# Paged-cache attention steps of a hybrid decoder: one piece of a dense projection moved to between two groups of small matmuls

## The chip, the cores and the metric

The kernel runs on 1 core of one Trainium2 chip. The metric is the device time of the whole launch in microseconds (us). The kernel is written engine by engine: TensorE (PE), VectorE (DVE), ScalarE (ACT), GpSimd (POOL) and SyncE (SP) each have an instruction list, and semaphores order them.

## What is computed

One layer of a decoder over 512 prompt tokens (with 16 meta tokens ahead) and 8 running sequences. Every layer has a gated-linear-attention group and a latent-attention group, then an output projection and a SwiGLU FFN. The change touches two parts: the attention of the 8 running sequences over their paged caches (4096 positions each), and the dense projections of the normed input into queries, keys and values of the linear-attention group.

```python
def page_step(carry, pages):                       # over the 32 pages of each sequence
    ck, kp = cache_ckv[layer, pages], cache_kpe[layer, pages]
    sc = (q_lat . ck + q_pe . kp) * MLA_SCALE      # scores, 4 heads
    m_new = maximum(m, sc.max(-1)); p = exp(sc - m_new)
    acc = acc * exp(m - m_new) + p @ ck            # values are the latent rows again
q, k, v, gr, g, cq, ckv, kpe = split(n @ w_in)     # q, k, v: the "dense pieces" below
```

## The kernel before

**The cache steps.** The caches are worked on in 16 steps, two for each of the 8 sequences (STEPS = 16). A step reads two halves, each of 128 partitions x 2048 latent elements (tile KC, 1 MB) and 128 x 512 rotary elements (KP, 256 KB), which POOL gathers from HBM by indirect DMA (L662 for KC, L669 for KP; the small copy L654 ahead of each pair writes the row numbers). They lie in a ring of six buffers, that is three steps. For half h, `gather_latent(h)` waits until the transposes of half h-6 are done and until the values matmuls of its step are done (semaphore pv_done, L661). So the two gathers of KC that POOL issues in step n are released by the values matmuls of step n-1, which PE runs inside step n.

Per step n the engines do this:

- DVE, in this order: `latent_keys(2n+1)` (L1911, transposes KC into KT), `rope_keys(2n+1)` (L1919, KP into KTp), `rope_keys(2n+2)` (waits for the scores of half 2n, since it writes their KTp), in steps 2, 7 and 13 also `lo(...)` (L1808, 2.25 us, the low part of the next weight block), then `cache_max(n)` (L1950 and L1952: the maximum over the scores, after both halves' scores), `latent_keys(2n+2)`, and `cache_probs(n)` (L1961, probabilities spread out for the values matmuls, writes PS).
- ACT: evacuates dense tiles that are complete, then `cache_exp(n)` (L1546, writes Pc after `cache_max(n)`).
- PE: two pieces of a dense projection, `cache_scores(n, 0)` (L991: 40 fp32 matmuls on tiles of 128x32, which the trace has as 80), `cache_values(n-1)` (L1014: 16 matmuls, 32 in the trace, also 128x32), `cache_scores(n, 1)`, then one or two more dense pieces, then `cache_spread(n)` (L1000: 4 matmuls of 128x128, after `cache_exp(n)`). The matmul that ends a group of scores raises sc_done, on which `cache_max` waits.

**The dense pieces.** `dense_piece(k)` is six matmuls, a part of a query, key (L934 to L936) or value (L815 to L817) tile. 92 pieces in all; pieces 0 to 15 run ahead of the steps, and `before_spread(n)` says how many are done before the spread of step n: three or four a step. They fill PE while it waits for DVE and ACT. Their matmuls use the whole 128x128 array.

**What sets the order.** Nothing but the text: the loop at L1018 to L1029 is PE's order, and PE runs it as it stands. DVE's, ACT's and POOL's orders are loops of their own and wait by semaphores.

```python
for n in range(STEPS):
    dense_piece(k)
    dense_piece(k + 1)
    cache_scores(n, 0)
    if n:
        cache_values(n - 1)
    cache_scores(n, 1)
    for k in range(k + 2, before_spread(n)):
        dense_piece(k)
    cache_spread(n)
    k = before_spread(n)
```

Of the kernel before, what the change touches and what calls it, by code (L numbers as in the profile page):

```python
# [240 lines left out]
def before_spread(n):  # L241

    return 16 + 4 * n + 4 - (n + 2) // 2 if n < STEPS else PIECES
# [13 lines left out]
def hybrid_decode_kernel(nc, ins, outs):  # L257
# [6 lines left out]
    with ExitStack() as ctx:  # L264
# [187 lines left out]
        def S(name):  # L452
            return signals[name]
# [302 lines left out]
        def _(pe):  # L756
# [220 lines left out]
            def cache_scores(n, y):  # L977

                if y == 0:
                    pe.wait_ge(S("kt_done"), 2 * n + 1)  # L980
                else:
                    pe.wait_ge(S("kt_first"), n + 1)
                if y == 0 and n >= 2:
                    pe.wait_ge(S("ps_done"), n - 1)
                o = 512 * (n % 2) + 64 * y
                for c in range(NBLK):
                    if y == 1 and c == 8:
                        pe.wait_ge(S("kt_done"), 2 * n + 2)
                    for t in range(NG):
                        kk = KT[y][:, 2 * t:2 * t + 2, c, :] if c < 8 else KTp[y][:, 2 * t:2 * t + 2, c - 8, :]  # L990
                        ins = mm(pairs[2][32 * t:32 * t + 32, o:o + 64], Qall[:, n // 2, 32 * c:32 * c + 32], kk, start=c == 0, stop=c == NBLK - 1)  # L991
                ins.then_inc(S("sc_done"), 1)

            def cache_spread(n):

                pe.wait_ge(S("sc_free"), n + 1)
                o = 512 * (n % 2) + P
                first16 = ident.rearrange("p (t a c) -> p a t c", t=NG, a=2)
                for v in range(4):
                    ins = nc.tensor.transpose(pairs[2][:, o + 64 * v:o + 64 * v + P], Pc[:, v, :, :].rearrange("p g j -> p (g j)"), first16)  # L1000
                ins.then_inc(S("sp_done"), 1)

            def cache_values(n):

                b = n // 2
                o = 512 * (b % 2)
                if n % 2 == 0 and b >= 2:
                    pe.wait_ge(S("ov_free"), b - 1)
                pe.wait_ge(S("ps_done"), n + 1)
                for v in range(4):  # L1010
                    x = (2 * n + v // 2) % RING
                    for t in range(NG):
                        unit = 2 * t + v % 2
                        ins = mm(pairs[3][32 * t:32 * t + 32, o:o + KVL], PS[n % 2][:, 4 * v + t, :], KC[x][:, KVL * unit:KVL * unit + KVL],  # L1014
                                 start=n % 2 == 0 and v == 0, stop=n % 2 == 1 and v == 3)
                ins.then_inc(S("pv_done"), 1)

            k = 16  # L1018
            for n in range(STEPS):
                dense_piece(k)  # L1020
                dense_piece(k + 1)
                cache_scores(n, 0)
                if n:
                    cache_values(n - 1)
                cache_scores(n, 1)
                for k in range(k + 2, before_spread(n)):
                    dense_piece(k)
                cache_spread(n)
                k = before_spread(n)  # L1029
# [1297 lines left out]
```

## Time and profile before

| | us |
|---|---|
| median of 3 runs | 880.56 |
| lowest, highest | 875.74, 881.65 |
| the profiled execution | 876.61 |
| its span, first to last instruction | 874.8 |
| PE busy | 794.5 (91%) |
| DVE busy | 445.6 (51%) |
| ACT busy | 270.6 (31%) |
| POOL busy | 124.1 (14%) |

The cache steps are the stretch from 111.3 us to about 290 us; ahead of them lie the norms and first projections, behind them prompt attention, the output projection and the FFN, where PE is busy without a break from 500 to 800 us. Times in the rows are from the first instruction. A PE row is the time at which the matmul was issued to the array and a modelled end, and PE rows run on while later ones wait; the releasers are read from semaphores.

### The profile page before, as it was taken

How to read it: one execution, taken by the hardware profiler on the slowest of the kernel's cores; microseconds unless marked ns; L12 is line 12 of the kernel's file. 1: busy time of each engine (PE TensorE's matmuls, PEld its weight loads, DVE VectorE, ACT ScalarE, POOL GpSimd, SP SyncE). 2: the span in 40 equal slices, each digit the busy share in tenths (PEclk: the TensorE clock that was granted, in tenths of full speed). 3: DMA queues.
4: the chain of work that ended last, by engine and by line, in shares of the span. 5: the costliest groups of instructions: out<-in, count | busy, mean ns of one | idle time of the engine just before them, and what ended most of it. 6: DMA issues, size and time to landing. Idle time of an engine off the chain costs nothing.

```text
span 874.8 us, 20180 instructions
## 1 busy us (share of the span) xinstructions
PE 794.5 (91%) x8841; PEld 750.6 (86%) x8841; DVE 445.6 (51%) x593; ACT 270.6 (31%) x429; POOL 124.1 (14%) x153
## 2 busy tenths in 40 slices
PE   2999888677769799999999999999999999999996
PEld 1999777566657589788999999999999999999996
DVE  5365567455557647779544555544445445123123
ACT  5346211111111534446534422222222223123213
POOL 6201414323332003622000000000000000000000
PEclk9999989978899999779999999999999999999999
DMA  9525556746763120231621322233333322322202
GB/s 260 170 56 175 214 210 244 262 153 238 290 242 137 49 73 5 57 97 51 200 84 47 105 83 78 87 95 96 96 96 96 96 85 67 114 97 85 84 0 97
DMA packets 72672, 106.52 MB, mean 122 GB/s; under 512 B 7808, under 2 KB 64216, under 8 KB 68384
## 3 DMA queue, kind: packets, MB, share of 16 engines
q1 hardware_dynamic: 64912, 63.42, 23.1%
q0 software_dynamic: 7696, 42.15, 13.1%
q8 instruction: 52, 0.85, 0.4%
q14 instruction: 12, 0.10, 0.0%
HBM read 101.03 MB, written 4.00 MB: 120 GB/s over the span
## 4 chain that ended last, share of the span: by engine, by line
PE 82%; DVE 5%; another core or an unknown queue 4%; issue 4%; ACT 3%; DMA 1%; SPq 0%; ACTq 0%; DVEq 0%
PE pair L797 10%; PE pair L799 10%; PE pair L798 10%; PE pair L782 8%; PE pair L784 8%; PE pair L783 8%; PE pair L991 4%; PE pair L1014 2%; PE pair L1213 1%; PE pair L815 1%; PE pair L817 1%; PE pair L816 1%; PE pair L835 1%; PE pair L1000 1%
## 5 line engine op out<-in xcount | busy, mean ns | idle before, releaser
L797 PE MATMUL pair<-xhi,whi 128*128 128x260 f32 x736 | 209.1, 284 | 0.4 <-ACT rsf L1736 0.4
L799 PE MATMUL pair<-xhi,wlo 128*128 128x260 f32 x736 | 208.5, 283 | 0.0
L798 PE MATMUL pair<-xlo,whi 128*128 128x260 f32 x736 | 208.5, 283 | 0.0
L797 PEld LDWEIGHTS pair<-xhi,whi 128*128 128x128 f32 x736 | 139.5, 190 | 0.7 <-issue 0.6
L798 PEld LDWEIGHTS pair<-xlo,whi 128*128 128x128 f32 x736 | 139.5, 190 | 0.0
L799 PEld LDWEIGHTS pair<-xhi,wlo 128*128 128x128 f32 x736 | 139.3, 189 | 0.0
L784 PE MATMUL pair<-hhi,wlo 128*128 128x260 f32 x352 | 99.4, 282 | 0.0
L782 PE MATMUL pair<-hhi,whi 128*128 128x260 f32 x352 | 99.3, 282 | 0.0
L783 PE MATMUL pair<-hlo,whi 128*128 128x260 f32 x352 | 99.2, 282 | 0.0
L1911 DVE STREAM_TRANSPOSE KT<-KC 128x2048 uint32<-128x2048 uint32 x32 | 73.7, 2302 | 0.0
L2266 DVE TENSOR_TENSOR wlo<-wraw,whi 128x2048 fp32r<-128x2048 f32 x22 | 50.4, 2293 | 38.7 <-ACT whi L1756 38.7
L782 PEld LDWEIGHTS pair<-hhi,whi 128*128 128x128 f32 x352 | 66.3, 188 | 0.0
L783 PEld LDWEIGHTS pair<-hlo,whi 128*128 128x128 f32 x352 | 66.2, 188 | 0.0
L784 PEld LDWEIGHTS pair<-hhi,wlo 128*128 128x128 f32 x352 | 66.1, 188 | 0.0
L2291 DVE TENSOR_TENSOR wlo<-wraw,whi 128x2048 fp32r<-128x2048 f32 (+1 forms) x10 | 20.8, 2079 | 75.9 <-ACT whi L1768 75.9
L1751 ACT ACTIVATE hhi<-fe 128x520 f32 x22 | 13.8, 640 | 106.7 <-DVE fe L2279 106.7
L662 POOL DMA_INDIRECT KC<-in_cache_ckv,icur x32 | 31.7, 992 | 103.7 <-PE pair L1014 98.0
L1000 PE MATMUL pair<-cst,Pc 128*128 128x128 f32 x64 | 13.0, 334 | 33.8 <-ACT Pc L1546 26.2
L991 PEld LDWEIGHTS pair<-KT,Qall 128*32 128x32 f32 x2048 | 36.7, 121 | 8.2 <-issue 4.4
L991 PE MATMUL pair<-KT,Qall 128*32 128x64 f32 x2048 | 40.8, 235 | 2.0 <-issue 1.7
L1000 PEld LDWEIGHTS pair<-cst,Pc 128*128 128x128 f32 x64 | 8.2, 164 | 39.8 <-ACT Pc L1546 31.5
L1756 ACT ACTIVATE whi<-wraw 128x2048 fp32r<-128x2048 f32 x22 | 41.8, 1901 | 0.0
(362 smaller groups left out, 1687.1 us busy)
## 6 DMA issues: line engine op xcount, KB each, us to landing
wraw<-in_w_gate SPq DMA_DIRECT2D x11, 1024.0 KB
wraw<-in_w_up SPq DMA_DIRECT2D x11, 1024.0 KB
wraw<-in_w_down SPq DMA_DIRECT2D x8, 1024.0 KB
X<-in_x_prompt SPq DMA_DIRECT2D x8, 512.0 KB, 5.7
wraw<-in_w_in SPq DMA_DIRECT2D x4, 1024.0 KB
wsame<-in_w_in SPq DMA_DIRECT2D x4, 1024.0 KB
wraw<-in_w_down SPq DMA_DIRECT2D x4, 768.0 KB
wsame<-in_w_out SPq DMA_DIRECT2D x2, 1024.0 KB
```

The costliest lines, as they stand in the source:

```text
L662: g.indirect_dma_start(KC[x][:, :], None, ckv_rows, bass.IndirectOffsetOnAxis(icur[x][:, 0:1], 0)).then_inc(S(f"kc_loaded{x}"), 16)
L782: mm(out, wcols(h, j), hi[:, kx, tok], start=first and j == 0, stop=False)
L783: mm(out, wcols(h, j), lo[:, kx, tok], start=False, stop=False)
L784: ins = mm(out, wcols(l, j), hi[:, kx, tok], start=False, stop=last and j == len(k_of) - 1)
L797: mm(out, h[:, k, c], xhi[:, k, tok], start=k == order[0], stop=False)
L798: mm(out, h[:, k, c], xlo[:, k, tok], start=False, stop=False)
L799: ins = mm(out, l[:, k, c], xhi[:, k, tok], start=False, stop=k == order[-1])
L991: ins = mm(pairs[2][32 * t:32 * t + 32, o:o + 64], Qall[:, n // 2, 32 * c:32 * c + 32], kk, start=c == 0, stop=c == NBLK - 1)
L1000: ins = nc.tensor.transpose(pairs[2][:, o + 64 * v:o + 64 * v + P], Pc[:, v, :, :].rearrange("p g j -> p (g j)"), first16)
L1756: f(whi[n % 2][:, :], wraw[n % 2][:, :], ACT.Copy).then_inc(w_hi, 1)
L1911: v_.transpose(KT[y][:, :, :, :].rearrange("p u c j -> p (u c j)").bitcast(U32), KC[x][:, :].bitcast(U32)).then_inc(S(signal), 1)
L2266: tt(wlo[n % 2][:, :], wraw[n % 2][:, :], whi[n % 2][:, :].bitcast(F32), ALU.subtract).then_inc(w_lo, 1)
```

## The change

In PE's loop the second of the two dense pieces at the head of each step goes from ahead of `cache_scores(n, 0)` to behind `cache_values(n - 1)`, just ahead of `cache_scores(n, 1)`. In step 0, which has no values, it stands between the two groups of scores.

```diff
             for n in range(STEPS):
                 dense_piece(k)
-                dense_piece(k + 1)
                 cache_scores(n, 0)
                 if n:
                     cache_values(n - 1)
+                dense_piece(k + 1)
                 cache_scores(n, 1)
                 for k in range(k + 2, before_spread(n)):
                     dense_piece(k)
```

On PE, at the middle of step 1, this is the place where the piece arrives (whi and wlo are the weight block, xhi and xlo the input, KT0/KTp0 and KT1/KTp1 the keys of the two halves, KC the values):

```order
@@ -579,4 +579,8 @@
 L935 MATMUL pair0<-xlo_50,whi1_52 128x268
 L936 MATMUL pair0<-xhi_49,wlo1_54 128x268
+L991 MATMUL pair2<-KT0_93,Qall_73 32x64 x32
+L991 MATMUL pair2<-KTp0_95,Qall_73 32x64 x8
+L1014 MATMUL pair3<-KC0_81,PS0_97 32x256 x8
+L1014 MATMUL pair3<-KC1_82,PS0_97 32x256 x8
 L934 MATMUL pair0<-xhi_49,whi1_52 128x268
 L935 MATMUL pair0<-xlo_50,whi1_52 128x268
```

The first half's scores and the values of the step before now come six dense matmuls earlier. On PE again, a few rows on, where the second half's scores begin:

```order
@@ -585,8 +589,4 @@
 L935 MATMUL pair0<-xlo_50,whi1_52 128x268
 L936 MATMUL pair0<-xhi_49,wlo1_54 128x268
-L991 MATMUL pair2<-KT0_93,Qall_73 32x64 x32
-L991 MATMUL pair2<-KTp0_95,Qall_73 32x64 x8
-L1014 MATMUL pair3<-KC0_81,PS0_97 32x256 x8
-L1014 MATMUL pair3<-KC1_82,PS0_97 32x256 x8
 L991 MATMUL pair2<-KT1_94,Qall_73 32x64 x32
 L991 MATMUL pair2<-KTp1_96,Qall_73 32x64 x8
```

There the dense piece stands directly ahead of the second half's scores, where the values stood before. No instruction is added or removed, and the lists of DVE, ACT, POOL and SP are the same as before.

## Rows read from the trace of the kernel before

**Rows 1.** Windows: two cache steps; busy us of each engine, then PEclk, DMA, GB/s.

```profile
160.20:173.70 13.50, 9.35 (x220) 8.06 (x220) 7.76 (x8) 1.11 (x5) 4.60 (x7) 0.87 0.66 235
...
269.10:277.30 8.20, 7.08 (x214) 5.95 (x214) 7.01 (x8) 1.42 (x4) 0.98 (x2) 1.00 0.82 309
```

**Rows 2.** Waits, 108 to 292 us: who waited for whom, us in total, times, longest.

```profile
POOL KC L662 <- PE pair L1014: 98.0, 13, 16.1
...
DVE fin L1950 <- remote: 47.4, 9, 7.1
```

**Rows 3.** Timeline of step 5: start, us, engine, line, idle before and releaser.

```profile
164.98 1.90 PE L1014 MATMUL pair<-KC,PS 128*32 128x256 f32 x32
...
166.71 1.07 PE L991 MATMUL pair<-KT,Qall 128*32 128x64 f32 x62
...
167.65 0.40 PE L991 MATMUL pair<-KTp,Qall 128*32 128x64 f32 x14
...
167.69 0.95 POOL L662 DMA_INDIRECT KC<-in_cache_ckv,icur  x1 [7.14 <-PE pair L1014]
...
171.23 0.29 DVE L1950 TENSOR_REDUCE fin<-pair 128x1 f32<-128x128 f32 x1 [5.21 <-remote]
```

**Rows 4.** Timeline of step 14, which issues no gather behind its values.

```profile
274.92 0.41 PE L991 MATMUL pair<-KTp,Qall 128*32 128x64 f32 x16
...
275.40 0.29 DVE L1950 TENSOR_REDUCE fin<-pair 128x1 f32<-128x128 f32 x1 [1.16 <-PE pair L991]
```

**Rows 5.** Timeline of steps 1, 2, 8 and 12: first gather and cache_max of each.

```profile
122.43 0.95 POOL L662 DMA_INDIRECT KC<-in_cache_ckv,icur  x1 [16.07 <-PE pair L1014]
...
125.95 0.29 DVE L1950 TENSOR_REDUCE fin<-pair 128x1 f32<-128x128 f32 x1 [4.87 <-remote]
...
134.53 1.32 POOL L662 DMA_INDIRECT KC<-in_cache_ckv,icur  x1 [7.00 <-PE pair L1014]
...
136.01 0.29 DVE L1950 TENSOR_REDUCE fin<-pair 128x1 f32<-128x128 f32 x1 [0.98 <-PE pair L991]
...
203.91 0.95 POOL L662 DMA_INDIRECT KC<-in_cache_ckv,icur  x1 [3.76 <-PE pair L1014]
...
209.72 0.29 DVE L1950 TENSOR_REDUCE fin<-pair 128x1 f32<-128x128 f32 x1 [7.14 <-remote]
...
253.34 0.95 POOL L662 DMA_INDIRECT KC<-in_cache_ckv,icur  x1 [5.63 <-PE pair L1014]
...
257.62 0.29 DVE L1950 TENSOR_REDUCE fin<-pair 128x1 f32<-128x128 f32 x1 [5.08 <-remote]
```

**Rows 6.** Timeline of PE in step 1, in and out of the small-tile matmuls.

```profile
118.23 0.28 PE L935 MATMUL pair<-xlo,whi 128*128 128x268 f32 x1
118.35 0.29 PE L936 MATMUL pair<-xhi,wlo 128*128 128x268 f32 x1
118.57 1.10 PE L991 MATMUL pair<-KT,Qall 128*32 128x64 f32 x64
...
122.33 0.41 PE L991 MATMUL pair<-KTp,Qall 128*32 128x64 f32 x16
122.67 0.39 PE L934 MATMUL pair<-xhi,whi 128*128 128x268 f32 x1
122.89 0.29 PE L935 MATMUL pair<-xlo,whi 128*128 128x268 f32 x1
```

**Rows 7.** Timeline of step 12, where the second half's scores are late.

```profile
254.37 0.43 PE L991 MATMUL pair<-KTp,Qall 128*32 128x64 f32 x15
```

**Rows 8.** Timeline of DVE and PE at the head of step 14.

```profile
268.21 2.31 DVE L1911 STREAM_TRANSPOSE KT<-KC 128x2048 uint32<-128x2048 uint32 x1
...
269.15 0.66 PE L1000 MATMUL pair<-cst,Pc 128*128 128x128 f32 x4 [0.71 <-ACT Pc L1546]
...
271.16 1.04 PE L991 MATMUL pair<-KT,Qall 128*32 128x64 f32 x60
```

**Rows 9.** The line of the latent gathers, whole run.

```profile
DMA to landing us min/median/max: 6.1/7.3/8.6
```

## Prediction

> **What bounds the kernel now.** I read the page first: PE is busy 91% of the span, but in its slices of 22 us the cache steps stand out, where PE is at 6 to 8 tenths. So I cut that stretch into windows, one per step. They come in two kinds [rows 1]: a step of the first kind takes 13.5 us for 9.35 us of PE work, one of the last three takes 8.2 us for 7.08 us. The work is the same. What differs is that the first kind issues gathers and the last ones do not (the latent halves 6 to 31 are gathered during steps 1 to 13, two a step).
>
> The waits say who is late [rows 2]. POOL's latent gathers wait 98 us for the values matmuls, and DVE's `cache_max` waits 47.4 us in nine steps for a releaser that the profile cannot match. The timeline of step 5 shows why it cannot [rows 3]. The values matmuls end at 164.98 + 1.90 = 166.88. The second half's scores are issued from 166.71 and end, by their rows, at 167.65 + 0.40 = 168.05. `cache_max` needs nothing else, yet starts at 171.23, 3.18 us later. In step 14, where no gather is issued, the same pair of rows gives 275.33 and 275.40, a lag of 0.07 us [rows 4]. So the scores' completion is held back in steps with gathers, and I call that time the hold.
>
> The hold is timed by POOL, not by PE. From the start of the first latent gather to `cache_max` it is 171.23 - 167.69 = 3.54 us in step 5 [rows 3] and 125.95 - 122.43 = 3.52 us in step 1 [rows 5]. Steps 1, 3, 4, 5, 6, 9, 10 and 11, eight in all, look alike. Step 8 has 5.81 us and step 12 has 4.28 us [rows 5]. In steps 2, 7 and 13 DVE is still on `lo` when the gather starts, the gather takes 1.32 us instead of 0.95, and the lag is only 136.01 - 134.53 = 1.48 us [rows 5]. Ten steps have the long hold; steps 0, 2, 7, 13, 14 and 15 do not.
>
> The path of a step is therefore: spread, the two dense pieces, scores, values, scores, the hold, `cache_max`, `cache_exp`, the next spread. All PE work ahead of the hold is on the path in series. The dense pieces behind the second scores hide under the hold and the ACT and DVE work.
>
> **The change, part by part.**
>
> *The piece itself.* It stays ahead of the second scores, so its six matmuls are on the path before and after. At full clock they follow each other by 118.35 - 118.23 = 0.12 us [rows 6], that is 6 x 0.12 = 0.73 us with rounding. Their net cost is nothing.
>
> *More changes between large and small tiles.* Before, a step goes from 128x128 matmuls to 128x32 ones and back once; after, twice. Going in costs 118.57 - 118.35 = 0.22 us where 0.12 is the pitch, so 0.10 [rows 6]. Coming out, the last small matmul starts at about 122.52 (122.33 + 0.41 less 0.22, a small matmul's length in the trace), a next one would follow in 0.05, and the dense one starts at 122.67: 0.10 more. The second dense matmul then comes after 0.22 instead of 0.12: again 0.10 [rows 6]. Together 0.30 us per step, and 16 x 0.30 = 4.8 us if every step pays it on the path. The Trainium skill, "TensorEngine Tiling (Array Packing)", section Key Properties, says that changing the tiling mode drains TensorE. If each of the two added changes waits out the rest of one dense matmul (0.29 less 0.12 us, from the same rows), that gives 0.34 us per step and 5.4 us; this rule speaks against the change, and the trace agrees with it in size.
>
> *The values end earlier.* They are issued six dense matmuls sooner, 0.73 us at full clock. Where the granted clock is at half (1.2 GHz) over that whole piece, it is up to twice that, 1.46 us. POOL starts its gather 167.69 - 166.88 = 0.81 us after them [rows 3], so the gather starts 0.73 us earlier too. At that moment PE has just finished the moved piece, and the second scores, 1.2 to 1.3 us of work, fall wholly behind the gather's start. Before, only about 0.4 us of them did.
>
> *What the hold then does* is the unknown term. No row has this exact order, so I bound it by neighbours. From below: `cache_max` still comes 3.52 us after the gather starts, so it comes 0.73 us sooner. From above: as in step 8, 5.81 us after it, so 5.81 - 3.52 - 0.73 = 1.56 us later. Nearest to the new order is step 12, where the scores' last rows end at 254.37 + 0.43 = 254.80, which is 1.46 us behind the gather's start at 253.34 [rows 5, 7]; after the change I expect about 0.73 - 0.81 + 1.30 + 0.30 = 1.5 us. There the lag was 4.28 us: 4.28 - 3.52 - 0.73 = +0.03 us per step. I take that value.
>
> *The keys of the first half come closer.* In step 14 the spread starts at 269.15 and the scores at 271.16 [rows 8]; with one piece less they want to start at 270.43. Their transpose ends at 268.21 + 2.31 = 270.52. So about 0.1 us may be lost ahead of the first scores; it is won back, as the same time is then missing ahead of the second. I count nothing, and up to 0.1 x 16 = 1.6 us as bound.
>
> *Gathers.* Issued sooner by 0.73 us, they land in 7.3 us [rows 9] and are transposed no earlier than a whole step, at least 8.2 us [rows 1], later. DVE's transposes L1911 wait for no landing in the steps. Nothing is won there. In steps 2, 7 and 13 `lo` and the gather both move ahead by about as much, so they still overlap; if they did not, these three would get the long lag, 3 x (3.52 - 1.48) = 6 us.
>
> *Sum.* Ten hold steps at +0.03 give +0.3 us, their tile changes being under the hold; six other steps at +0.30 give +1.8 us. The profiled execution took 876.61 us, so 876.61 + 2.1 = 878.7 us. The median of the runs shown is 3.95 us above that execution; on its scale the forecast is 880.56 + 2.1, rounded to 882.5 us.
>
> **The rivals.**
>
> 1. *The hold has a fixed end, 3.52 us behind the gather.* For it: eight steps of ten agree to 0.06 us, although their scores were not all equally far. Against it: the two steps whose scores were latest broke it. Time: 10 x (-0.73) + 1.8 = -5.5 us, 875.1 us; with the piece at half clock throughout, 10 x (-1.46) + 1.8 = -12.8, 867.8 us.
> 2. *The hold has a fixed length behind the scores' own end.* Then only the tile changes count, in all 16 steps: +4.8 us, 885.4 us. For it: the lag is near 3.2 us in most. Against it: steps 8 and 12 have less behind their own ends.
> 3. *The hold gets longer, as in step 8.* What decides is how much of the second scores lies behind the gather's start: 0.4 us in step 5, all of it after the change. If that stretches every hold as in step 8, it is 10 x 1.56 + 1.8 = +17.4 us, 898.0 us. For it: step 8 itself. Against it: step 12, whose lateness is the nearer to the new order's, lost less.
> 4. *The hold disappears*, because it needs values and scores in one unbroken stretch. Then each of ten steps gains up to 3.1 us, less 4.8 us of tile changes: -26 us, 854.6 us. DVE would allow it, as the 8.2 us step shows. The steps with `lo` speak for it weakly, since there too the hold is cut when something on another engine shifts.
>
> **How the numbers follow.** I give the forecast 0.36, rival 1 0.21 (0.05 of it at half clock), rival 2 0.16, rival 3 0.15, rival 4 0.07, and 0.05 to the rest. Runs of before spread from 875.74 to 881.65, so about 1% (8.8 us) is what a measurement can tell from no change. Faster by over 1%: rival 4, the half-clock part of rival 1 and a little of the rest, 0.14. Slower: rival 3 and some of the rest, 0.18. Same: 0.68. The range 872 to 894 holds the forecast, rival 2, rival 1 at full clock and a third of rival 3; left out are rival 4, the far end of rival 1 and the worse part of rival 3, about 0.2.
>
> **What would show it.** In the changed profile, six dense rows should stand between L1014 and the second L991 of each step, and L662 should start about 0.8 us behind the end of L1014. Right if the lag from the first L662 to L1950 is 4.1 to 4.5 us in the ten steps and 1.5 us in steps 2, 7 and 13. Near 3.5 us is rival 1, near 5.8 us is rival 3, under 2 us is rival 4. If the lag from the scores' rows to L1950 is 3.2 us everywhere, it is rival 2. In steps 0, 14 and 15 the time should grow by 0.3 us each; if it does not, the tile changes are mis-sized. Wrong altogether if the last kind of step gets shorter, for then PE's series was not the path.

## The result, and the profile after

| us | before | changed |
|---|---|---|
| median of the comparison | 881.07 | 899.68 |
| lowest, highest | 875.74, 881.65 | 897.93, 901.46 |
| span of the profiled execution | 874.8 | 896.9 |

The ratio is 1.0206, with a 95% interval from 1.0163 to 1.0249. The forecast was 882.5 us and no measurable change, the range ended at 894: the prediction is wrong. The time nearest to the measured one is that of rival 3, 898.0 us. The medians differ by 18.6 us and the two profiled executions by 22.1 us (876.61 and 898.68), because the profiled one of before is 4.5 us under its median; what is read from the traces below adds up to the second figure.

There is a second half to this result. On most other chips the same pair of kernels goes the other way. The study is about both.

First the windows of the changed kernel, a step with gathers (step 4) and the one without (step 14), from spread to spread; the columns are those of [rows 1]. The first line is step 4 of before.

```profile
148.50:160.20 11.70, 8.15 (x216) 6.94 (x214) 6.45 (x8) 1.64 (x5) 4.23 (x7) 0.91 0.89 315
...
155.00:168.30 13.30, 10.40 (x216) 7.81 (x214) 5.15 (x8) 1.78 (x4) 4.23 (x6) 0.88 0.48 170
290.60:299.50 8.90, 7.70 (x214) 6.48 (x214) 6.48 (x8) 1.44 (x4) 1.30 (x2) 1.00 0.83 308
```

PE's busy time in step 4 grew from 8.15 to 10.40 us although no instruction was added, and the step without gathers takes 8.9 us where it took 8.2 [rows 1]. The waits from 108 to 310 us, as in [rows 2]:

```profile
POOL KC L662 <- PE pair L1014: 119.1, 13, 15.3
DVE fin L1950 <- PE pair L991: 79.1, 14, 7.8
...
PEld pair L991 <- issue: 41.6, 77, 0.6
...
PE pair L991 <- issue: 29.2, 72, 0.4
```

`cache_max` no longer waits for a releaser that the profile can't match. It waits for L991 itself, and L991 stops 72 times inside its own group, for nothing that the profile shows, 0.4 us at most each time. The timeline of step 4 shows how:

```profile
159.24 0.83 PE L1014 MATMUL pair<-KC,PS 128*32 128x256 f32 x12
...
160.72 0.28 PE L936 MATMUL pair<-xhi,wlo 128*128 128x268 f32 x1
160.88 0.95 POOL L662 DMA_INDIRECT KC<-in_cache_ckv,icur  x1 [9.76 <-PE pair L1014]
...
160.94 0.87 PE L991 MATMUL pair<-KT,Qall 128*32 128x64 f32 x46
...
162.16 0.34 PE L991 MATMUL pair<-KT,Qall 128*32 128x64 f32 x5 [0.35 <-issue]
...
162.92 0.34 PE L991 MATMUL pair<-KT,Qall 128*32 128x64 f32 x5 [0.42 <-issue]
...
163.67 0.34 PE L991 MATMUL pair<-KT,Qall 128*32 128x64 f32 x6 [0.42 <-issue]
...
164.99 0.98 POOL L669 DMA_INDIRECT KP<-in_cache_kpe,icur  x1 [0.27 <-POOL icur L654]
...
166.69 0.24 PE L991 MATMUL pair<-KTp,Qall 128*32 128x64 f32 x1 [0.43 <-issue]
...
166.98 0.29 DVE L1950 TENSOR_REDUCE fin<-pair 128x1 f32<-128x128 f32 x1 [7.00 <-PE pair L991]
```

The values end at 160.07, the gather follows 0.81 us later, and the rows of 46 of the 80 small matmuls follow without a stop. From then on PE gets five or six through every 0.75 us, until 166.69; POOL's four gathers last until 164.99 + 0.98 = 165.97. I call this the trickle. From the first gather to `cache_max` it is 166.98 - 160.88 = 6.10 us. In steps 1, 3 to 6 and 8 to 12 the lag lies between 6.08 and 6.30 us; step 7 has 3.97. In steps 2 and 13, where `lo` lengthens the first gather, it stays short:

```profile
136.39 1.69 POOL L662 DMA_INDIRECT KC<-in_cache_ckv,icur  x1 [10.05 <-PE pair L1014]
...
138.27 0.29 DVE L1950 TENSOR_REDUCE fin<-pair 128x1 f32<-128x128 f32 x1 [1.02 <-PE pair L991]
```

The account of the loss has four parts, each the difference between the two traces. The lags of steps 1 to 13 grew by 26.4 us in all. The stretches from a spread to the next first latent gather shrank by 12.3 us, a little more than 13 pieces of 0.73 us. The stretches from `cache_max` to the next spread grew by 7.6 us. Steps 14 and 15, which have no gather behind their values, grew by 0.67 and 0.37 us (from one first L1000 row to the next, 8.22 to 8.89 and 8.92 to 9.29). The sum is 22.8 us, and from the spread of step 0 to that of step 15 the stage grew from 170.2 to 193.0 us.

The third part is one that the prediction had put under the hold. The dense pieces behind the second scores now stand behind the trickle, and they run at the lower of the two clocks. In step 1 they begin at 127.31, `cache_max` at 127.42, and the granted clock of the window behind is 0.50:

```profile
127.31 0.59 PE L934 MATMUL pair<-xhi,whi 128*128 128x268 f32 x1
127.42 0.29 DVE L1950 TENSOR_REDUCE fin<-pair 128x1 f32<-128x128 f32 x1 [6.60 <-PE pair L991]
```

```profile
127.30:130.10 2.80, 2.80 (x13) 2.79 (x13) 2.64 (x3) 0.78 (x2) 0.00 (x0) 0.50 0.91 376
```

Twelve of them, 0.22 us apart where they are 0.12 apart at full clock, keep PE busy until the spread at 130.16, 2.74 us after `cache_max`. In step 1 of before the same stretch is 1.35 us long and PE has nothing left to do in it. So it is in steps 1, 3, 9 and 11, 4.7 of the 7.6 us. In steps 6, 7 and 13, 3.2 us, `cache_exp` itself starts later, and why I have not traced.

### The profile page after: what moved, and what is told of

Read it like the earlier page. It is cut to its first block, busy times and chain, and to the rows that moved or that the text cites. A ratio compares the mean times of both kernels' runs of the same rounds, so it can differ in the third digit from the quotient of the medians.

```text
span 896.9 us, 20180 instructions
## 1 busy us (share of the span) xinstructions
PE 819.7 (91%) x8841; PEld 759.9 (85%) x8841; DVE 445.4 (50%) x593; ACT 270.4 (30%) x429; POOL 124.9 (14%) x153
## 4 chain that ended last, share of the span: by engine, by line
PE 86%; issue 5%; DVE 3%; ACT 2%; another core or an unknown queue 2%; DMA 1%; SPq 0%; ACTq 0%; DVEq 0%
PE pair L797 10%; PE pair L799 10%; PE pair L798 10%; PE pair L782 8%; PE pair L784 8%; PE pair L783 7%; PE pair L991 7%; PE pair L1014 3%; PE pair L815 2%; PE pair L816 2%; PE pair L817 2%; PE pair L1000 1%; PE pair L1213 1%; PE pair L1145 1%
## 5 line engine op out<-in xcount | busy, mean ns | idle before, releaser
L797 PEld LDWEIGHTS pair<-xhi,whi 128*128 128x128 f32 x736 | 139.2, 189 | 0.7 <-issue 0.6
L991 PE MATMUL pair<-KT,Qall 128*32 128x64 f32 x2048 | 48.9, 229 | 17.7 <-issue 17.7
L991 PEld LDWEIGHTS pair<-KT,Qall 128*32 128x32 f32 x2048 | 36.5, 115 | 29.8 <-issue 26.1
L1950 DVE TENSOR_REDUCE fin<-pair 128x1 f32<-128x128 f32 x16 | 4.7, 292 | 82.6 <-PE pair L991 79.1
L815 PE MATMUL pair<-whi,xhi 128*128 128x256 f32 x120 | 42.6, 355 | 0.4 <-issue 0.4
```

The costliest lines, as they stand in the source:

```text
L797: mm(out, h[:, k, c], xhi[:, k, tok], start=k == order[0], stop=False)
L815: mm(out, hi[:, tok], wcols(h, j), start=j == 0, stop=False)
```

## Experiments

The hypotheses at the start: **A**, while GpSimd issues gathers, PE gets small matmuls through only in a trickle; **C**, it is the gathers' traffic; **D**, the added tile changes (from 128x128 matmuls to 128x32 ones and back) cost the whole 18 us. **B**, the order of the work as such, came beside them. Later came **F**, that PE waits for its own instructions.

The stage is the time from the first L1000 matmul of step 0 to that of step 15. The last column is worked out from the traces and explained further down: the breaks of more than 0.5 us from one matmul row to the next for which the profile shows no releaser and which end at the edge of a block of PE's instructions, behind a packet that brings instructions. Both columns are of the one profiled execution, which in after_third took 838.04 us, 6.8 us less than its median.

| kernel | chip | us | ratio to before, interval | stage | such breaks, us |
|---|---|---|---|---|---|
| before, changed | first | 881.07, 899.68 | 1.0206, 1.0163 to 1.0249 | 170.2, 193.0 | 6.0, 0 |
| late_gather | 7 | 847.74 | 1.0009, 0.9972 to 1.0046 | 146.1 | 18.7 |
| late_gather_moved | 7 | 842.69 | 0.9940, 0.9900 to 0.9979 | 141.9 | 15.3 |
| piece_before_values | 7 | 845.82 | 0.9966, 0.9936 to 0.9997 | 145.3 | 17.8 |
| small_gather | 7 | 835.09 | one execution | 132.9 | 5.7 |
| before_again | 13 | 848.41 | | 145.5 | 20.2 |
| after_again | 13 | 844.38 | 0.9964, 0.9939 to 0.9989 | 143.8 | 13.8 |
| hardware_loads | 13 | 848.58 | 1.0012, 0.9980 to 1.0044 | 144.8 | 15.6 |
| half_the_small_matmuls | 13 | 830.93 | one execution | 132.3 | 10.1 |
| half_the_columns | 13 | 841.90 | 0.9932, 0.9891 to 0.9973 | 140.8 | 14.2 |
| after_fourth | 13 | 841.29 | 0.9934, 0.9892 to 0.9976 | 140.2 | 13.5 |
| after_third | 6 | 844.81 | 0.9984, 0.9955 to 1.0012 | 139.2 | 13.6 |
| late_gather_moved_second | 6 | 844.49 | 0.9953, 0.9928 to 0.9977 | 142.9 | 14.5 |
| late_gather_moved_third | 8 | 846.17 | 0.9971, 0.9942 to 1.0000 | 142.5 | 12.9 |
| after_fifth | 10 | 898.06 | 1.0274, 1.0197 to 1.0350 | 191.7 | 1.0 |
| small_gather_timed | 10 | 898.54 | 1.0278, 1.0208 to 1.0348 | 192.1 | 0.8 |
| small_gather_before | 10 | 877.92 | 0.9995, 0.9963 to 1.0028 | 170.1 | 2.0 |
| late_gather_moved_fourth | 10 | 875.09 | 0.9893, 0.9822 to 0.9965 | 169.9 | 0.9 |
| hardware_loads_second | 9 | 848.48 | 0.9691, 0.9636 to 0.9746 | 145.1 | 15.1 |

The kernel before itself took 849.64 us on chip 7, 848.41 and 849.26 on 13, 847.37 on 6, 847.29 on 8, but 878.76 and 883.13 on 10 and 874.10 on 9. So there are two kinds of chip for this kernel. I call 6, 7, 8 and 13 ordinary, and 9, 10 and that of the first measurement the trickling kind. The kernel before itself was traced on the first chip and on 13 only; elsewhere its time tells which kind a chip is. Of the 28.2 us between the spans of before_again and of the first trace, 24.7 lie in the stage (145.5 against 170.2).

### A later gather, and another place for the piece

In late_gather the latent gather waits for the second scores too (order of before); late_gather_moved has the same in the changed order. piece_before_values leaves the gather and puts the piece between the first scores and the values; its lines below are against the changed kernel.

```diff
                     pool.wait_ge(S("pv_done"), (h - RING) // 2 + 1)
+                    pool.wait_ge(S("sc_done"), 2 * ((h - RING) // 2 + 1) + 2)
```

```diff
                 cache_scores(n, 0)
+                dense_piece(k + 1)
                 if n:
                     cache_values(n - 1)
-                dense_piece(k + 1)
                 cache_scores(n, 1)
```

> The order of before; POOL's first latent gather of a step waits for the second half's scores too, not only for the values. Theory A (while POOL issues its gathers, PE gets through small matmuls only at about five in 0.75 us, so what counts is how many of them lie behind the first gather's start): no score is left behind the gather, the lag from the scores' last row to cache_max falls from 3.2 us to under 0.2 us in the ten hold steps, and the kernel is 20 to 30 us faster than before. Theory B (the hold comes from the order of matmuls on PE, wherever POOL is): the lag stays at 3 us, no change. Theory C (the transferred data slow PE, not their issue): the transfers now meet the next step's first scores, so these get longer by what the second scores gain, no change within 5 us.

> The same late gather, with the piece moved as in the change. Theory A: the change then costs only its two added changes between large and small tiles, 0.3 us in 16 steps: 4 to 6 us slower than the late gather with the order of before, and still clearly faster than before. Theory B: it stays 18 us slower than its partner, and the second scores take 6 us from the gather's start. Theory D (the tile changes themselves cost the 18 us): the same 18 us.

> The moved piece stands between the first half's scores and the values, so values, second scores and gathers keep before's order and distance, but the two added tile changes are there. Theory A: the hold is as before, 3.5 us from gather to cache_max; only 0.3 us x 16 = 5 us are lost. Theory D (tile changes): about as slow as the change, +18 us.

All three ran on chip 7, where by its time the kernel before has next to no hold to remove, so A's 20 to 30 us, its hold of 3.5 us and its cost of 4 to 6 us all missed, and the three say little on A, B and C. late_gather is no different from before, 1.0009. late_gather_moved is 0.6% faster. piece_before_values is 0.3% faster, with lags from 0.69 to 2.69 us, where 3.5 was the pattern of the first trace. What they did show: an order with more tile changes in every step does not cost 18 us by itself (piece_before_values 0.9966, late_gather_moved 0.9940), and steps 14 and 15 of the first comparison agree (0.67 and 0.37 us). D fell.

### A quarter of the gathers' bytes

```diff
-                g.indirect_dma_start(KC[x][:, :], None, ckv_rows, ...)
+                g.indirect_dma_start(KC[x][:, 0:512] if h >= RING else KC[x][:, :], None,
+                                     kpe_rows if h >= RING else ckv_rows, ...)
```

> The changed kernel, but the latent gathers of halves 6 to 31 read rows of 512 elements instead of 2048, so POOL issues as many gathers of as many rows with a quarter of the latent bytes; three quarters of the values and keys are stale. Theory A: the second scores still take 5 us or more from the gather's start. Theory C (traffic): that time falls to under 3 us.

> The order of the changed kernel; from the seventh half on the latent gathers fetch rows of 512 elements from the rotary cache in place of 2048 from the latent cache (a quarter of the bytes, the same number of gathers), so the latents of those halves are not the reference's. Theory F (TensorE waits for its own instructions, because their packets come late behind the gathers' traffic): 833 to 838 us and under 6 us of such waits in the cache steps. If it is the issuing of gathers by GpSimd, whatever their size, 842 to 845 as in the changed kernel.

> The order of the kernel before, with the same small gathers. Theory F: the waits for instruction packets fall from 18 us to under 7 us, so it takes 830 to 838 us, and the changed order has lost its advantage: small_gather_timed against this one lies between 0 and +0.7% (16 pieces with four tile changes more a step, 0.30 us each, are 4.8 us, 0.6%). If the advantage of the changed order has nothing to do with those waits, this kernel is 0.2 to 0.7% slower than small_gather_timed.

The latents of these halves are not the cache's, so this is a kernel for timing only. On chip 7 the changed order took 835.09 us with them, in one execution; the changed kernel itself was not timed there, and on the other ordinary chips it took 841 to 845. Its lags are 1.41 to 2.24 us. This misses A's 5 us and looks like C's "under 3", but the changed kernel on an ordinary chip has 1.42 to 4.17 us (after_again), so there was no trickle to remove. On chip 10 nothing happened: 898.54 against 898.06 us in the changed order, 877.92 against 878.76 in the order of before. What was expected of the last two runs, made for an ordinary chip, missed, so for F small_gather's one execution is the only run with fewer bytes. (The second expectation counts four added tile changes a step; there are two, for 0.30 us together.) The timeline of step 4 of small_gather_timed has the same trickle:

```profile
157.39 0.95 POOL L662 DMA_INDIRECT KC<-in_cache_kpe,icur  x1 [9.10 <-PE pair L1014]
...
157.45 0.87 PE L991 MATMUL pair<-KT,Qall 128*32 128x64 f32 x46
...
159.44 0.33 PE L991 MATMUL pair<-KT,Qall 128*32 128x64 f32 x5 [0.42 <-issue]
...
160.17 0.33 PE L991 MATMUL pair<-KT,Qall 128*32 128x64 f32 x6 [0.40 <-issue]
...
163.43 0.29 DVE L1950 TENSOR_REDUCE fin<-pair 128x1 f32<-128x128 f32 x1 [6.79 <-PE pair L991]
```

Five or six per 0.73 us, and a lag of 6.04 us, at a DMA rate of 92 GB/s from 108 us to the end of the stage in place of 201. Over the stage GpSimd's queue moved 13.4 MB in 4080 packets in place of 33.8 MB in 5744. C is refuted for the trickle, as far as it is a matter of bytes.

### The two kernels again

> The kernel before, unchanged, profiled on the chip on which the other experiments run. On that chip the kernel before took 849.64 us in 25 executions, 31 us less than in the first profile, whose rows carry the prediction. Theory A (while GpSimd issues its four gathers, TensorE gets through only about five small matmuls in 0.75 us) says that the 31 us lie in the cache steps: the lag from the first gather of a step to cache_max, 3.5 us in eight of the first fifteen steps, should be under 1.5 us here, and the sixteen steps together 20 to 30 us shorter. Theory D (the machine is just faster as a whole) says that the lags stay at 3.5 and that every stage is about 3.5% shorter.

> The changed kernel, unchanged, on the same chip. If what the change costs is the time that small matmuls lose behind a gather's start (theory A), it costs there as much as that loss is present on this chip: between -0.5% (none of it: the six later pieces only fill other places) and +2% (as in the first measurement), with the lag of the first gather to cache_max above that of the kernel before in most steps. If it is the eight tile changes a step themselves (theory D: 18 us over 16 steps, whatever GpSimd does), it is +2% here too, 867 us, and the kernel with the same order and a later gather, which took 0.994 of the time before, would not have come out so.

> The changed kernel, unchanged, on whichever chip this job gets. Theory M (what the change costs depends on how much small matmuls are slowed behind a gather's start, and that differs between chips): if the kernel before takes 870 to 885 us here, the change costs 1.5 to 2.5% and the lags from first gather to cache_max are about 6.1 us in ten steps; if the kernel before takes about 849 us, it costs between -1% and 0 and most lags are 1.4 to 3.2 us. Rival (the +2% of the first measurement comes with the order of the work, and the second measurement at 0.996 was the odd one): +1.5 to +2.5% here wherever the kernel before stands.

> The changed kernel, unchanged, beside half_the_columns. If the kernel before takes about 849 us here, the changed kernel takes 0.994 to 1.001 of it, as on the three chips so far; if it takes 870 to 885, the ratio is 1.015 to 1.025 and the lags from the first gather to cache_max are about 6.1 us.

> The changed kernel, unchanged. If the kernel before takes about 849 us here, the changed kernel takes 0.993 to 0.999 of it; if it takes 870 to 885, the ratio is 1.015 to 1.025, with ten lags of about 6.1 us.

On ordinary chips the changed kernel is 0.9964, 0.9984 and 0.9934 of the kernel before: a gain of 0.2 to 0.7%, of which one interval takes in 1. On chip 10 it is 1.0274, with lags of 5.92 to 6.06 us in steps 1 and 3 to 12. The first measurement was no accident, and the sign of this change depends on the chip. The interval on chip 10 overlaps with that of the first measurement. Two of the expected ratios were narrowly missed: 0.9934 where 0.994 to 1.001 was expected, and 1.0274 where 1.015 to 1.025 was; both intervals reach into the expected range. In before_again the stage was 24.7 us shorter, as A expected, but only nine of its thirteen lags are under 1.5 us; the other four are taken up below.

### Holding the gather back on a trickling chip

> The order of the changed kernel, the latent gather held back until the second half's scores are done, on the same chip as after_third. Theory A (GpSimd's issuing of gathers slows the small matmuls behind it): 840 to 848 us on any chip, because no small matmul of the scores stands behind a gather's start; on a chip where the kernel before takes 870 to 885 that is a ratio of 0.955 to 0.975, elsewhere 0.99 to 1.0. Rival (the chip is slower as a whole): the ratio to the kernel before is 0.99 to 1.0 on every chip, so 870 or more where the kernel before takes 880.

> The order of the changed kernel, the latent gather held back until the second half's scores are done. Where the kernel before takes 870 to 885 us: theory A (GpSimd's issuing of gathers slows small matmuls behind it) expects 842 to 855 us, a ratio of 0.96 to 0.98, and scores that end 0.1 us before cache_max in every step; a rival (such a chip slows the cache steps' matmuls as such, or only moves the slow time behind the new place of the gather) expects 0.99 to 1.02. Where the kernel before takes about 849 us: 0.993 to 0.998, as on chips 7 and 6.

> The same kernel as late_gather_moved_third, for a chip of the slower kind. Where the kernel before takes 870 to 885 us: theory A expects 842 to 855 us and scores that end 0.1 us before cache_max; the rival (the slow time only moves behind the gather's new place) 0.99 to 1.02 of the kernel before. Where the kernel before takes about 849 us: 0.993 to 0.998.

The second and third ran on ordinary chips (0.9953, 0.9971), the fourth on chip 10: 875.09 us, 0.9893 of the kernel before. My expectation of 842 to 855 us was wrong, and the rival, that the slow time only moves, came nearest with its 0.99 to 1.02. The timeline of its steps 3 and 4 (line numbers are one higher here) shows it. The first gather has started at 148.40, behind the scores of step 3. The first half's scores of step 4 begin at 150.40:

```profile
150.40 1.13 PE L992 MATMUL pair<-KT,Qall 128*32 128x64 f32 x43
...
151.10 0.95 POOL L663 DMA_INDIRECT KC<-in_cache_ckv,icur  x1 [0.30 <-issue]
...
151.96 0.32 PE L992 MATMUL pair<-KT,Qall 128*32 128x64 f32 x6 [0.43 <-issue]
...
152.53 0.97 POOL L670 DMA_INDIRECT KP<-in_cache_kpe,icur  x1 [0.27 <-POOL icur L654]
152.72 0.33 PE L992 MATMUL pair<-KT,Qall 128*32 128x64 f32 x5 [0.43 <-issue]
...
153.46 0.32 PE L992 MATMUL pair<-KT,Qall 128*32 128x64 f32 x5 [0.41 <-issue]
...
154.35 0.37 PE L992 MATMUL pair<-KTp,Qall 128*32 128x64 f32 x12
```

The trickle is now in the other half's scores, behind the second latent gather. It stops at about 154.3, 0.8 us after the end of the last gather, 152.53 + 0.97, and the rows that are left follow without a stop. This is the closest view of A: the trickle moved with the gathers and ended with them. That it is shorter because only some of the gathers meet small matmuls is my reading. The view has a limit. Gathers are being issued from 148.40 on, yet 43 rows from 150.40 on show no stop (46 in step 4 of the changed kernel), and since PE's rows can run ahead of its completions, the rows do not tell when the slowing begins. The stage is 169.9 us, where the changed kernel has 191.7 on this chip.

### No gathers by GpSimd

hardware_loads has the changed order. The loops of gathers on POOL are gone; ScalarE issues plain transfers of the same size at the matching points: in both traces the first KC transfer of a step is issued 0.4 to 0.8 us after the values end, ahead of the second half's scores. The kernel leaves out the page table and reads the rows in the order of the cache.

```diff
+            def load_half(h):
+                x = h % RING
+                act.dma_start(KP[x][:, :], flat_kpe[P * h:P * h + P, :]).then_inc(S(f"kp_loaded{x}"), 16)
+                act.dma_start(KC[x][:, :], flat_ckv[P * h:P * h + P, :]).then_inc(S(f"kc_loaded{x}"), 16)
...
+                if 1 <= n <= 13:
+                    act.wait_ge(S("pv_done"), n)
+                    for h in (2 * n + 4, 2 * n + 5):
+                        act.wait_ge(S("kt_done"), h - RING + 1)
+                        load_half(h)
```

> The order of the changed kernel; latents and rotary rows of all halves are loaded by plain transfers that ScalarE issues (the same bytes into the same buffers, at the same points: after the step's scores and transposes), and GpSimd issues no gather in the cache steps. It reads the rows in their order in the cache, without the page table, so the values differ from the reference's. Theory A (what slows small matmuls is GpSimd issuing indirect transfers): the lag of the first load to cache_max is that of the matmuls alone, below 1.6 us, no groups of five with gaps, and the time is 25 us or more under the kernel before's of the first profile, at 0.98 to 0.995 of the kernel before on the same chip. Theory C (the traffic of 0.6 MB into SBUF slows TensorE's reads): the lags stay as in the changed kernel on this chip, and the time too.

> The same kernel as hardware_loads: the changed order, rows loaded in their order in the cache by transfers that ScalarE issues, no gather of GpSimd in the cache steps, so the values differ from the reference's. Where the kernel before takes 870 to 885 us: if the slow matmuls come with GpSimd's issuing, 843 to 855 us, a ratio of 0.96 to 0.98, and no scores in groups of five or six; if they come with any transfer into these buffers, 890 to 900 us with such groups. Where the kernel before takes about 849 us: 0.998 to 1.005, as on chip 13.

On ordinary chip 13: 848.58 us, 1.0012. On chip 9, where the kernel before took 874.10 us: 848.48 us, 0.9691 with an interval from 0.9636 to 0.9746. With the same bytes into the same buffers but no gathers from GpSimd, the kernel takes the same time on either kind of chip. This settles A against C. What it leaves open is whether the engine that issues counts or the kind of transfer (indirect gathers against plain ones, over another queue), since both changed together. The timeline of step 4 on chip 9, the transfers and the scores (L979 here):

```profile
149.86 0.34 ACTq L1521 DMA_DIRECT2D KP<-in_cache_kpe  x1
150.22 1.36 ACTq L1522 DMA_DIRECT2D KC<-in_cache_ckv  x1
```

```profile
150.60 1.10 PE L979 MATMUL pair<-KT,Qall 128*32 128x64 f32 x64
151.52 0.41 PE L979 MATMUL pair<-KTp,Qall 128*32 128x64 f32 x16
```

All 80 in one run, straight behind two transfers. From the first KC transfer to `cache_max` it is 1.77 us here and 1.46 to 1.86 in the other steps without a break (A had expected less than 1.6). In the whole stage of this trace PE makes no stop of over 0.5 us without a releaser but the ten in the table's last column. The changed kernel itself was not timed on chip 9, so the 3.1% are against the kernel before. On chip 13, hardware_loads is about as slow as before, though the changed order alone is 0.4 to 0.7% faster (it was expected at 0.98 to 0.995); what ScalarE's issuing costs there was not traced. (The 0.6 MB in the first expectation is a slip: a half is 1.25 MB.)

### Where the ordinary chips lose and gain

The trace of before_again raised a new question: its lags run from 0.68 to 3.36 us, and PE has a few long breaks instead of a trickle. Its PE rows in steps 5 and 10:

```profile
158.22 0.61 PE L991 MATMUL pair<-KT,Qall 128*32 128x64 f32 x27
161.14 0.55 PE L991 MATMUL pair<-KT,Qall 128*32 128x64 f32 x25 [2.31 <-issue]
```

```profile
210.66 0.28 PE L816 MATMUL pair<-whi,xlo 128*128 128x256 f32 x1
213.10 0.37 PE L817 MATMUL pair<-wlo,xhi 128*128 128x256 f32 x1 [2.16 <-issue]
```

The second break is between two dense matmuls, so it has nothing to do with tile size. The DMA view of a short window at each place, 158.6 to 158.7 and 210.70 to 210.75, shows what else started:

```profile
q8 instruction: 1, 0.02, 68.7%
```

```profile
q8 instruction: 1, 0.02, 126.0%
```

In each it is one packet of the instruction queue, 16 KB (0.85 MB in 52 packets over the whole run). By the trace these two start at 158.64 and 210.72, and PE is back 2.50 and 2.38 us later. PE waits for its own instructions there, because it has used them up before the next packet has come (F). The trace shows it in a second way. Between the first L1000 rows of steps 0 and 15 PE has 6547 rows, counted with weight loads and the few other instructions of its list, and 26 packets of queue 8 start: about 252 rows to a packet, so 256 is the natural count. Number PE's rows from the first, and take every break of over 0.5 us that has no releaser. In the 14 traces without a trickle there are 143 of them, and every one ends at row 193 or 194 of a block of 256. 133 of the 143 end 2.2 to 2.6 us after a packet starts, the rest within 2.1 to 3.1 us. The short stops of the trickle are another thing: of the 72 in the changed kernel's first trace not one ends so behind a packet. These sums are the last column of the table. The step has two groups of 80 matmuls with 160 instructions in 1.3 us each, weights and matmuls, with only the values between them in the old order.

The Trainium skill, "Runtime: NRT & Kernel Launch", section Instruction fetch mechanics, says that crossing to a new 16 KiB block is mostly hidden. Here the trace disagrees: 13 to 20 us of the stage on ordinary chips, with the full gathers or loads.

Two kernels in the changed order test F. Both leave out half of the second half's scores. half_the_small_matmuls makes them with half of the matmuls (five of ten blocks, 40 of 80 in the trace; the expectation says nine and 72, which is a slip), half_the_columns keeps their number and halves their columns.

```diff
-                for c in range(NBLK):
+                for c in (range(NBLK) if y == 0 else (0, 1, 2, 3, 8)):
```

```diff
+                        if y == 1:
+                            ins = mm(pairs[2][32 * t:32 * t + 32, o:o + 32], Qall[:, n // 2, 32 * c:32 * c + 32], kk[:, 0:1, :], ...)
+                            continue
```

> The order of the changed kernel; the second half's scores are made of five of nine contraction blocks (40 small matmuls of 72; the first half's stay), so that part of the scores is left out. Theory A, with n matmuls left behind the first gather's start at 0.15 us each (0.75 us for five): where the lag of the changed kernel on this chip is above 1.5 us, it falls by nearly half. Theory B (the order of the work alone; the lag is a fixed wait after the gather, whatever stands behind it): the lag stays.

> The order of the changed kernel; each matmul of the second half's scores takes 32 columns in place of 64, so half of the keys of that half get no scores, but the number of TensorE's instructions stays. Theory F (in the cache steps TensorE waits for its own instructions: on the three chips so far its longest gaps end 2.3 to 2.5 us after a 16 KB packet of the instruction queue starts, and the steps with 144 instructions in 1.1 us use a packet up faster than that): the gaps stay, and the time is within 0.5% of the changed kernel's 842 to 845 us, where half the matmuls gave 830.9. Rival (TensorE's time in the scores sets the end): halving the columns gives what halving the matmuls gave, 830 to 836 us.

Half the columns: 841.90 us beside the changed kernel's 841.29 on the same chip, breaks 14.2 us beside 13.5, as F expects. The columns are not free, since steps 14 and 15 became 0.43 and 0.42 us shorter (8.14 and 8.87 beside 8.57 and 9.29); why the whole did not become shorter I have not traced. Half the matmuls: 830.93 us in one execution, 10.4 to 13.5 us under the changed kernel on that chip, and breaks 10.1 us, only 3.4 to 3.7 us less. The larger part is work in series: a lag without a break is 0.90 us in place of 1.44, and 16 x 0.54 is 8.6 us, an estimate. So this run fits F and is no proof of it. The same fits the table: with a quarter of the gathers' bytes on chip 7 the breaks are 5.7 us instead of 13.5 to 13.8. There the traffic counts, unlike for the trickle. That the packets then come sooner was not measured by itself.

F also fits the gain on ordinary chips. The dense piece between values and second scores spreads PE's instructions: breaks 20.2 and 18.7 us in the old order, 13.8, 13.5 and 13.6 in the new. The stage is 145.5 and 146.1 us in the old, 139.2 to 143.8 in the new. But the tile changes cost something as well: steps 14 and 15 grew by 0.34 and 0.33 us on chip 13. They did not cost that in every step. Steps 4 and 6 have gathers and no break in either trace of that chip (before_again, after_again), and they grew by 0.07 and 0.04 us only. With one trace to a run, and 1.7 to 6.3 us between their stages, the account of the gain is a fit and not shown. On trickling chips such breaks are 0 to 6 us in all kernels with gathers.

## Why the prediction was wrong, step by step

- **The path of a step** had the hold in series on it, and that was right: the grown lags show up in the stage. Its last sentence was not. The dense pieces behind the second scores were to hide under the hold, and in the changed kernel they ran behind `cache_max`, at a granted clock near 0.50 in most steps: 4.7 us of the 7.6 us that these stretches grew. Two smaller readings were off as well: the page has PE at 9 tenths in the slice from 262 to 284 us, not at 6 to 8, and 13.5 us is the longest of the steps with gathers, which run from 10.05 to 13.44.
- **The piece at no cost**: six dense rows stand between L1014 and the second L991, and the gather starts 0.81 us behind the values, as before. Right.
- **Tile changes, 0.30 us a step**: measured 0.67 and 0.37 in steps 14 and 15 of the first comparison, 0.34 and 0.33 on chip 13. Slightly low for a step without gathers. The rule of the Trainium skill ("TensorEngine Tiling (Array Packing)", Key Properties), worked out there as 0.34 us, as an estimate hits the figures of chip 13. That these changes hide under the hold in steps with gathers was given without a reason, as they lie ahead of the gather's start. Chip 13 has +0.07 and +0.04 us in two such steps, so there they hardly cost anything; for the trickling chips it is not shown.
- **What the hold then does, +0.03 us a step**, is the step that failed. The lag was to be 4.1 to 4.5 us and was 6.08 to 6.30. In step 4 that is 6.10 - 3.53 - 0.73 = +1.84 us instead of +0.03; over the ten steps the lags grew by 23.5 us, which less ten times 0.73 is +1.62 us a step (step 8 had -0.35, because its lag was 5.81 us already in the kernel before). Two things were wrong in it. I took the neighbour by the time at which the scores' last row ends, and step 12 looked nearest. But step 12's rows were late by a break of 1.14 us at a block edge (F), and step 3 contradicts the measure: its last score row ends 2.73 us behind the gather, after a break of 2.4 us, later than step 12's 1.46, and its lag is still 3.51 us:

```profile
146.24 0.22 PE L991 MATMUL pair<-KTp,Qall 128*32 128x64 f32 x1 [2.19 <-issue]
```

So rival 1's "the two steps whose scores were latest" was misread too; they were 8 and 3. And I took the hold for a delay of the completion alone, whose length hardly depends on what is behind the gather. In the changed kernel's rows it looks like a rate: at five or six matmuls per 0.75 us, the 34 that are left when the trickle begins need 34 / 5.6 x 0.75 = 4.6 us. In step 8 of before, with the lag of 5.81 us [rows 5], 34 of the 80 rows lie behind the gather's start, where steps 1, 4, 6, 10 and 11 have 8. Its PE rows between 204 and 208 us would have shown the groups of five and six, and I had read only its ends. The rate is not the whole of it: on chip 10 the lag is 5.92 to 6.06 us in eleven steps, though the last score row starts anywhere from 2.98 to 5.80 us behind the gather.

- **Rival 3** named the right point, how much of the scores lies behind the gather's start, and its price of 1.56 us a step came within 0.1 us of the mean of +1.62. It had 0.15. That its sum of 898.0 us lies 1.7 us from the median is in part luck: it has nothing for the dense pieces behind `cache_max`, for step 7's longer lag or for a gather that starts more than 0.73 us sooner, and it is set beside medians 18.6 us apart where the profiled pair has 22.1.
- **Steps 2, 7 and 13**: near in 2 and right in 13 (1.88 and 1.44 us). Step 7 has 3.97, 2.5 us more than before; the prediction had named such a loss (2 us for each of the three steps) and counted nothing for it.
- **Rival 1 and rival 2**: the hold's end was not fixed at 3.52 us, nor its length at 3.2 us behind the rows (0.04 us in most steps). On ordinary chips there is hardly a hold at all, so rival 4's mechanism is nearer there, but at 0.993 to 0.998 and not at 26 us, since the kernel before has no hold to lose either.
- **Not thought of at all**: that the hold, on which the whole sum rested, belongs to one kind of chip. One trace could not have told it.

Of the kernels run, the changed order with the late gather was below the kernel before on all four chips: 0.9940, 0.9953, 0.9971 (its interval ends at 1.0000) and, on a trickling one, 0.9893. That last is 2.6% less than the changed kernel there (875.09 against 898.06 us), or 3.7% by the two ratios; the kernel before, timed beside each, took 883.13 and 878.76 us. It is the version to keep, with the gain on the ordinary chips under 1%. The late gather in the old order was never timed on a trickling chip.

What stays open: why some chips trickle and others not; what PE and GpSimd contend for there; why the old order shows a fixed 3.5 us; and why `lo` beside the gather shortens it. The one common trait is that the first gather itself then takes longer. In the three trickling traces of the new order with the early gather (after, after_fifth, small_gather_timed), a first gather of 0.95 us goes with a lag of 5.9 to 6.3 us, one of 1.10 with 5.92, one of 1.32 with 3.97 and 3.89, and one of 1.69 to 2.29 with 1.4 to 2.0.

## What to carry to other kernels

When a wait has no visible releaser, look at the rate of the waiting engine's own rows in the step where the wait is longest, not only at its ends: a delay can turn out to be a rate, and then what you move behind it is multiplied. On a chip like these three, keep groups of many tiny matmuls away from the time in which GpSimd issues indirect transfers, and on a chip without the trickle spread them between dense work, since PE used up its instructions in them faster than the next packet came; that the spreading is what gained is a fit here. And where a change is worth under 3%, time it on more than one chip before believing its sign.

## What the runs showed of the hardware that was not expected

- Chips differ by 3 to 4% on the same kernel (847 to 850 against 874 to 883 us), most of it in one stage (24.7 of 28.2 us in the one pair of traces), through the slowing of small matmuls behind GpSimd's gathers: five or six per 0.75 us. Without such gathers both kinds take 848.5 us (one chip of each).
- This slowing doesn't depend on the bytes of the gathers (201 and 92 GB/s, 898.06 and 898.54 us).
- PE can wait over 2 us for its instructions, at the edge of a block of 256 of them (143 breaks of 143), and resumes mostly 2.2 to 2.6 us after the 16 KB packet starts; in 16 steps that was 13 to 20 us on ordinary chips. With fewer bytes in the gathers it was 5.7 us, with fewer instructions 10.1 us.
- Behind a trickle the granted clock was 0.50, and the dense matmuls that came next stood 0.22 us apart instead of 0.12.
